# Keys, queries and values of the last attention projected from tiles that carry only their norm weight

## The chip, the cores and the metric

The program runs on one core of one Trainium2 chip. The metric is the device time of one execution in microseconds (us), the median of several. Everything is float32. Five engines work side by side and wait for each other through semaphores: TensorE (PE; its weight loads are listed as PEld), VectorE (DVE), ScalarE (ACT), GpSimd (POOL) and SyncE (SP), which issues most transfers.

## What is computed

The reference is a chain of two transformer blocks of two layers each over 512 tokens of 1024 features. Only the last layer of the second block is touched. It normalises the residual `h` twice, once for keys and values and once for queries, projects, normalises every head of 128, and attends:

```python
def rms_norm(x, g):
    y = x32 * lax.rsqrt(jnp.mean(x32 * x32, axis=-1, keepdims=True) + EPS)
    return (y * g.astype(jnp.float32)).astype(x.dtype)

hn = rms_norm(h, kv_norm)
kv = (hn @ w_kv).reshape(B, S, N_GROUPS, 2, KV_HEADS, HEAD_DIM_2)
k, v = kv[:, :, :, 0], kv[:, :, :, 1]
k = rms_norm(k, k_norm[:, None, :])
...
q = (rms_norm(h, b_norm) @ w_q).reshape(B, S, N_GROUPS, Q_HEADS, HEAD_DIM_2)
q = rms_norm(q, q_norm[:, None, :])
```

A token's factor r = 1/sqrt(mean(h^2) + EPS) passes through the projection. Call the head without it k'. Then the head's own norm gives k' r / sqrt(mean(k'^2) r^2 + EPS) = k' / sqrt(mean(k'^2) + EPS (mean(h^2) + EPS)). So a key or query head needs no factor r: the guard of its root becomes EPS times the token's squared root. A value has no head norm and must be multiplied by r.

## The kernel before

The residual lies in `X`, 8 tiles (k) of 128 features by tokens; columns CTX to TOK are the 512 tokens. The parts of the program that matter here follow each other on TensorE:

- **SW0**, a `fast_stage`: the gated MLP of the layer before. A slot is one weight tile of 1024 KB in a ring of three. `fast_stage` computes a slot as seven products of blocks (Strassen's scheme), numbered 1 to 7; TensorE runs 1, 2, 5, 6, 3, 7, then product 1 of the next slot, then 4. The last four slots (s = 0 to 3) each finish two of the eight tiles of `X`, halves of 256 tokens at a time. DVE does that in `to_residual`: behind product 2, 3 and 7 it adds the product to a copy that ACT made (L1989, L1985), adds the sum to `X` (L1927), squares the half (L1940) and adds the square to a running sum (L1955); behind product 4 it adds straight to `X`. TensorE's product 4 waits for `c22_done`, the add behind product 7.
- **norm(6)**: TensorE multiplies the summed squares by a column of ones (`column`, L793), which gives the sum of each token down a column of PSUM. ACT takes the root (`std`, L1411), DVE the reciprocal (L1832), TensorE spreads it along the partitions (L818), and DVE writes `H` = `X` times weight times root (L1857), one tile at a time. It then copies the spread root to `rstd_s` (L2485) and writes `HKP`, the same product in the order of four phases (L2487).
- **Keys**: three slots of `project` (L665), two units of 8 matmuls each, first from `H`, then from `HKP`. ACT copies a finished unit to `K2` and squares it (`head_tile`, L1713, L1714). The next slot's weights are fetched when an earlier one is done.
- **Values**: three slots of `project_tokens` (L772), copied to `V2` by ACT (L1751). Meanwhile DVE writes `H` anew from `X`, `b_norm` and `rstd_s` (L2518).
- **HEADS**, a `fast_stage` of 12 slots: the query heads. Between products, groups of heads have their squares summed (`group_sums`, `group_turn`), and ACT takes the roots of the collected columns in `small` in three calls of `roots` (L1740): behind slot 1, behind slot 9, and ahead of the attention.
- **dilated_attention**: 32 units in a chain DVE, ACT, TensorE. ACT loads the table of the exponential ahead of the first.

Each engine's program is written out in order by hand; nothing reorders it.

## Time and profile before

| | us |
|---|---|
| median of 3 runs | 3467.29 |
| lowest, highest | 3465.44, 3472.61 |
| the profiled execution | 3469.39 |
| its span, first to last instruction | 3467.8 |

| engine | busy us | share of the span |
|---|---|---|
| PE | 3337.5 | 96% |
| DVE | 2006.7 | 58% |
| POOL | 1019.0 | 29% |
| ACT | 720.5 | 21% |

A matmul in float32 leaves two records in the trace, so a unit of `project` is 16 records. A record's duration overlaps with the next one's; how far apart they start is the cost of a row of them. Matmul times are modelled. Gaps are more telling: a bracket at the end of a row of the timeline is the time in which the engine stood idle ahead of it, and who ended that.

### The profile page before, as it was taken

How to read it: one execution, taken by the hardware profiler on the slowest of the kernel's cores; microseconds unless marked ns; L12 is line 12 of the kernel's file. 1: busy time of each engine (PE TensorE's matmuls, PEld its weight loads, DVE VectorE, ACT ScalarE, POOL GpSimd, SP SyncE). 2: the span in 40 equal slices, each digit the busy share in tenths (PEclk: the TensorE clock that was granted, in tenths of full speed). 3: DMA queues.
4: the chain of work that ended last, by engine and by line, in shares of the span. 5: the costliest groups of instructions: out<-in, count | busy, mean ns of one | idle time of the engine just before them, and what ended most of it. 6: DMA issues, size and time to landing. Idle time of an engine off the chain costs nothing. (4 is left out here: it accounts for less than half of the span.)

```text
span 3467.8 us, 39911 instructions
## 1 busy us (share of the span) xinstructions
PE 3337.5 (96%) x15432; PEld 2475.8 (71%) x15432; DVE 2006.7 (58%) x3518; ACT 720.5 (21%) x1548; POOL 1019.0 (29%) x800
## 2 busy tenths in 40 slices
PE   5999999999999999999999999999999998999998
PEld 4567775555555556778888854888886885678887
DVE  7666467766665443277445657654444676665543
ACT  2243231000101234131111124111111233311110
POOL 0110222322333000223444401344441650234443
PEclk9999999999999999999999999999999999999999
DMA  6332422333321121231222221222222220022222
GB/s 260 108 111 79 114 57 73 118 113 121 116 90 57 65 71 50 70 89 63 88 89 89 87 73 62 75 94 86 85 97 85 80 86 25 26 73 87 93 89 85
DMA packets 63580, 301.70 MB, mean 87 GB/s; under 512 B 7232, under 2 KB 19648, under 8 KB 37280
## 3 DMA queue, kind: packets, MB, share of 16 engines
q1 hardware_dynamic: 51872, 260.87, 22.3%
q0 software_dynamic: 6528, 18.75, 1.7%
q10 hardware_dynamic: 4992, 19.53, 1.5%
q8 instruction: 123, 2.02, 0.2%
q14 instruction: 65, 0.53, 0.1%
HBM read 294.27 MB, written 2.88 MB: 86 GB/s over the span
## 5 line engine op out<-in xcount | busy, mean ns | idle before, releaser
L2580 POOL TENSOR_TENSOR scratch<-ring 128x512 f32<-128x512 f32 (+1 forms) x160 | 214.2, 1339 | 1560.3 <-PE psum L694 1240.9
L694 PE MATMUL psum<-big,scratch 128*128 128x256 f32 (+1 forms) x2240 | 605.6, 426 | 0.0
L694 PEld LDWEIGHTS psum<-big,scratch 128*128 128x128 f32 x2240 | 425.6, 190 | 163.7
L694 PE MATMUL psum<-H,scratch 128*128 128x256 f32 (+1 forms) x2144 | 500.6, 388 | 3.4 <-ACT cb L1344 3.4
L694 PEld LDWEIGHTS psum<-H,scratch 128*128 128x128 f32 x2144 | 405.0, 190 | 84.7 <-ACT cb L1344 8.6
L694 PE MATMUL psum<-big,ring 128*128 128x256 f32 (+1 forms) x1584 | 427.7, 423 | 15.7 <-DVE big L2019 4.9
L665 PE MATMUL psum<-H,ring 128*128 128x512 f32 x928 | 424.2, 608 | 13.4 <-ACT H L1426 11.5
L694 PE MATMUL psum<-H,ring 128*128 128x256 f32 (+1 forms) x1536 | 403.7, 407 | 8.3 <-ACT H L1426 4.2
L694 PEld LDWEIGHTS psum<-big,ring 128*128 128x128 f32 x1584 | 302.6, 192 | 125.8 <-issue 7.2
L694 PEld LDWEIGHTS psum<-H,ring 128*128 128x128 f32 x1536 | 297.4, 194 | 84.4 <-issue 9.4
L665 PEld LDWEIGHTS psum<-H,ring 128*128 128x128 f32 x928 | 175.2, 194 | 222.7 <-issue 217.5
L1344 ACT ACTIVATE cb<-psum 128x256 f32<-128x256 f32 x336 | 128.5, 383 | 849.7 <-PE psum L694 849.7
L2581 POOL TENSOR_TENSOR scratch<-ring 128x512 f32<-128x512 f32 (+1 forms) x160 | 227.4, 1421 | 0.0
L2583 POOL TENSOR_TENSOR scratch<-scratch,ring 128x512 f32<-128x512 f32 (+1 forms) x160 | 225.2, 1407 | 0.0
L2585 POOL TENSOR_TENSOR scratch<-ring,scratch 128x512 f32<-128x512 f32 (+1 forms) x160 | 218.1, 1363 | 12.6
L1344 ACT ACTIVATE big<-psum 128x384 f32<-128x384 f32 x108 | 53.0, 491 | 540.0 <-PE psum L694 540.0
L694 PE MATMUL psum<-X,ring 128*128 128x256 f32 x672 | 159.5, 380 | 3.0 <-DVE cb L1985 1.6
L1989 DVE TENSOR_TENSOR cb<-psum,cb 128x256 f32<-128x256 f32 x104 | 44.0, 423 | 203.0 <-PE psum L694 202.9
L1803 DVE SCALAR_TENSOR_TENSOR big<-big,cb 128x1024 f32<-128x1024 f32 x128 | 158.7, 1259 | 3.1 <-DVE big L1803 2.8
L694 PE MATMUL psum<-X,scratch 128*128 128x256 f32 x672 | 158.7, 379 | 0.0
L2036 DVE TENSOR_TENSOR big<-psum,cb 128x256 f32<-128x256 f32 x88 | 37.2, 422 | 194.7 <-PE psum L694 194.7
L694 PEld LDWEIGHTS psum<-X,ring 128*128 128x128 f32 x672 | 126.7, 190 | 22.4 <-DVE big L1972 2.9
(361 smaller groups left out, 4143.8 us busy)
## 6 DMA issues: line engine op xcount, KB each, us to landing
ring<-in_wall SPq DMA_DIRECT2D x202, 1024.0 KB, 4.9
big<-in_wada SPq DMA_DIRECT2D x48, 512.0 KB, 3.6
big<-in_wada POOLq DMA_DIRECT2D x32, 512.0 KB, 3.9
big<-in_wada ACTq DMA_DIRECT2D x4, 2048.0 KB, 20.1
scratch<-in_rpb ACTq DMA_DIRECT2D x16, 512.0 KB, 4.4
X<-in_xin SPq DMA_DIRECT2D x4, 768.0 KB, 11.9
scratch<-negd SPq DMA_DIRECT2D x8, 384.0 KB, 8.3
big<-negd SPq DMA_DIRECT2D x8, 384.0 KB, 10.9
```

Source lines behind the costliest of these rows:

```text
L665: mm = pe.matmul(acc(w.unit), slot_cols(r, k, f * P, P), rhs_x(k), start=k == 0, stop=k == 7)
L694: mm = pe.matmul(fast_bank(st, q, b), lhsT, rhs(k), start=start and k == 0, stop=k == kt - 1, skip_group_check=True)
L1344: act.activation(piece(st, p, q), fast_bank(st, q, b), ACT.Copy).then_inc(copied[i], 1)
L1803: own(dve.scalar_tensor_tensor(out, w_tile, 1.0, cb[:, j * D:(j + 1) * D], ALU.mult, ALU.mult, accum_out=sums[:, 2 * r + j:2 * r + j + 1]))
L1989: step(dve.tensor_tensor(c, fast_bank(st, q, b), c, ALU.add))
L2036: step(dve.tensor_tensor(GS[s % 2][a], fast_bank(st, q, (0, 2)[x]), piece(st, x, q), ALU.add))
L2580: pool.tensor_tensor(s1, a21, a22, ALU.add).then_inc(combo_own, 1)
L2581: pool.tensor_tensor(s3, a11, a21, ALU.subtract)
L2583: pool.tensor_tensor(s2, s1, a11, ALU.subtract).then_inc(combo_own, 1)
L2585: pool.tensor_tensor(s4, a12, s2, ALU.subtract).then_inc(combos_ready, 1)
```

## The change

Four edits that belong together.

1. The tiles are multiplied by their norm weight alone. DVE writes `H` in `gain_tile`, within the last four slots of SW0: one tile behind the half of product 3, the other behind product 4. `HKP` and, later, the queries' `H` are written by `tensor_scalar` instead of `scalar_tensor_tensor`. The copy to `rstd_s` and the spreading of the root over the partitions (L818, 4 matmuls) are gone.
2. TensorE starts the keys' first slot when the last `c21_done` has come, and sums the tokens' squares behind its first unit (`token_squares`). The sums are now needed in two orders of tokens: 6 columns of 128 tokens, and 12 of 64 tokens, which gather each fourth column of the squares.
3. ACT takes the tokens' roots behind the second unit of keys (`token_roots`). DVE makes EPS times the squared root (the guard) and the reciprocal. `roots` has one instruction for each of the four token blocks, with the guard as bias, where it had one in all.
4. The copy of a value unit is split into two of 256 columns, each scaled by the tokens' reciprocal.

TensorE at the end of SW0 and the start of the keys (`scratch` and `num_b` hold the squares, `con` the identity, `H` and `ring` the operands of `project`):

```order
 L694 MATMUL psum<-big,ring 128x256 x3
-L793 MATMUL psum<-ones,scratch 128x1 x4
-L793 MATMUL psum<-ones,num_b 128x1 x2
-L818 MATMUL psum<-con,small 128x128 x4
-L665 MATMUL psum<-H,ring 128x512 x16
+L665 MATMUL psum<-H,ring 128x512 x8
+L1245 MATMUL psum<-ones,scratch 128x1 x2
+L1245 MATMUL psum<-ones,scratch 64x1 x4
+L1245 MATMUL psum<-ones,scratch 128x1 x2
+L1245 MATMUL psum<-ones,scratch 64x1 x4
+L1245 MATMUL psum<-ones,num_b 128x1 x2
+L1245 MATMUL psum<-ones,num_b 64x1 x4
```

Six sums and four spreading matmuls ahead of the first unit have become eighteen sums between the first and the second.

DVE in the last slot of SW0, from the update of `X` behind product 3, before:

```order
L1985 TENSOR_TENSOR cb<-psum,cb 128x256
L1927 TENSOR_TENSOR X<-cb,X 128x256
L1940 TENSOR_TENSOR aT<-X 128x256
L1955 TENSOR_TENSOR scratch<-scratch,aT 128x256
L1927 TENSOR_TENSOR X<-psum,X 128x256
L1940 TENSOR_TENSOR num_b<-X 128x256
L1832 RECIPROCAL small<-small 128x4
L1857 SCALAR_TENSOR_TENSOR H<-X,vec,psum 128x512 x8
```

and after:

```order
L1991 TENSOR_TENSOR scratch<-scratch,aT 128x256
L2003 TENSOR_SCALAR H<-X,vec 128x512
L2027 TENSOR_TENSOR cb<-psum,cb 128x256
L1963 TENSOR_TENSOR X<-cb,X 128x256
L1976 TENSOR_TENSOR aT<-X 128x256
L1991 TENSOR_TENSOR scratch<-scratch,aT 128x256
L1963 TENSOR_TENSOR X<-psum,X 128x256
L2003 TENSOR_SCALAR H<-X,vec 128x512
L1976 TENSOR_TENSOR num_b<-X 128x256
L2530 TENSOR_SCALAR big<-X,vec 128x512 x8
```

One tile is now written ahead of the add behind product 7 (L2027), one between the last update of `X` and its square.

ACT ahead of the attention (`small` holds the sums of the heads' squares, then their roots), before:

```order
L1729 ACTIVATE big<-psum 128x512
L1735 ACTIVATE small<-psum 128x8
L1740 ACTIVATE small<-small,eps_t 128x24
L1574 ACT_TABLE_LOAD
L1574 ACTIVATE scratch,small<-scratch,small 128x512 x2
```

and after:

```order
L1754 ACTIVATE big<-psum 128x512
L1760 ACTIVATE small<-psum 128x8
L1768 ACTIVATE small<-small 128x6 x4
L1595 ACT_TABLE_LOAD
L1595 ACTIVATE scratch,small<-scratch,small 128x512 x2
```

One root instruction ahead of the table load has become four.

The diff:

```diff
--- before.py
+++ after.py
@@ -1235,8 +1235,28 @@
             fast_stage(SW0)
 
 
-            norm(6)
+            pe.wait_ge(c21_done, w.fast)
             u_k = w.unit
+
+            def token_squares():
+
+                def column(t, at, squares, first=False):
+                    c, n = 6 * 512 + t, squares.shape[-1]
+                    return pe.matmul(psum[at:at + n, c:c + 1], squares, ones[:, 0:1], start=first, stop=True,
+                                     skip_group_check=True)
+
+                def columns(part, a, first=False):
+                    for j in range(2):
+                        column(2 + 2 * a + j, 0, part[:, j * P:(j + 1) * P], first and j == 0)
+                    for q in range(DIL):
+                        mm = column(6 + q, 64 * a, part[:, 0:256].rearrange("p (j q) -> p q j", q=DIL)[:, q, :])
+                    return mm
+
+                pe.wait_ge(sums_made, 6)
+                for a in range(2):
+                    columns(sq_sum[a], a, a == 0)
+                pe.wait_ge(last_squared, 6)
+                columns(sq_part[0], 0).then_inc(ssq_ready, 1)
 
             def group_sums(g):
 
@@ -1278,7 +1298,7 @@
                 if s == 1:
                     pe.wait_ge(h_ready, 8 * 8)
                 project(xq if s == 0 else lambda k: HKP[:, k, :], normed=48 if s == 0 else None,
-                        after=sums_between(0) if s == 2 else None)
+                        after=sums_between(0) if s == 2 else (lambda f: token_squares() if f == 0 else None) if s == 0 else None)
             project_tokens(lambda k, t: H[:, k, t * P:(t + 1) * P], False)
             for s in range(2):
                 project_tokens(lambda k, t: HKP[:, k, (t - CT) * P:(t - CT + 1) * P], False)
@@ -1371,9 +1391,10 @@
                         act.wait_ge(c21_done, q + 1)
                         query_head(q, s, 1)
                         if s == 1:
-                            roots(200, 224)
+                            roots(200, 208, 32)
+                            roots(208, 224).then_inc(q_std, 1)
                         if s == 9:
-                            roots(224, 296)
+                            roots(224, 296).then_inc(q_std, 1)
                     if st.kind == "relu" and kind == "in":
                         act.wait_ge(prod[4], q + 1)
                         act.activation(hid_half(st, 4 + s, 0), fast_bank(st, q, 1), ACT.Relu).then_inc(c21_done, 1)
@@ -1705,7 +1726,11 @@
 
             act.wait_ge(c21_done, w.fast)
             act.dma_start(M2, mask2).then_inc(mask2_in, 16)
-            std(6)
+
+            def token_roots():
+
+                act.wait_ge(ssq_ready, 7)
+                act.activation(small[:, 16:24], psum[:, 3074:3082], ACT.Sqrt, bias=eps_t[:, 0:1], scale=1.0 / D).then_inc(std_done, 1)
 
             def head_tile(i, f):
 
@@ -1736,26 +1761,37 @@
                                bank(7).rearrange("p (t j c) -> p j t c", t=XT, j=4)[:, 0:n, :, 0], ACT.Copy).then_inc(q_cols_out, 1)
                 act.wait_ge(q_cols_out, g + 1)
 
-            def roots(c0, c1):
-                act.activation(small[:, c0:c1], small[:, c0:c1], ACT.Sqrt, bias=eps_t[:, 0:1], scale=1.0 / P).then_inc(q_std, 1)
+            def roots(c0, c1, guard=36):
+
+                cols = small[:, c0:c1].rearrange("p (j t) -> p t j", t=XT)
+                for t in range(XT):
+                    ins = act.activation(cols[:, t, :], cols[:, t, :], ACT.Sqrt, bias=small[:, guard + t:guard + t + 1],
+                                         scale=1.0 / P)
+                return ins
 
             for s in range(3):
                 for f in range(2):
                     head_tile(2 * s + f, f)
+                    if s == 0 and f == 1:
+                        token_roots()
                     if s == 2:
                         (sum_columns if f else sum_rows)(0)
                 w.slot += 1
             for s in range(3):
                 for f in range(2):
                     half(f)
-                    act.activation(V2[:, s, 2 * f:2 * f + 2, :], acc(w.unit).rearrange("p (t c) -> p t c", t=2),
-                                   ACT.Copy).then_inc(acc_free[w.unit % 2], 1)
+                    act.wait_ge(diag_done, 7)
+                    for i in range(2):
+                        c = (24 if s == 0 else 28) + 2 * f + i
+                        ins = act.activation(V2[:, s, 2 * f + i, :], acc(w.unit)[:, 256 * i:256 * (i + 1)], ACT.Copy,
+                                             scale=small[:, c:c + 1])
+                    ins.then_inc(acc_free[w.unit % 2], 1)
                     w.unit += 1
                 w.slot += 1
             fast_stage(HEADS)
             sum_rows(7)
             sum_columns(7)
-            roots(296, 320)
+            roots(296, 320).then_inc(q_std, 1)
             dilated_attention()
             turned_y(8, DT, lambda i: 1.0, False,
                      lambda i, s: (H[:, i, CTX:TOK].rearrange("p (j q) -> p q j", q=DIL),
@@ -1843,7 +1879,7 @@
 
                 if n:
                     inverse(n)
-                dve.wait_ge(rstd_ready, n + 1)
+                dve.wait_ge(rstd_ready, n + 1 - (n > 6))
                 for k in range(DT):
                     if n < 4:
                         a = gain
@@ -1961,6 +1997,12 @@
                                 own.wait()
                                 dve.sem_inc(sums_made, 1)
 
+                def gain_tile(k):
+
+                    if st is SW0:
+                        dve.tensor_scalar(H[:, k, CTX:TOK], X[:, k, CTX:TOK], v("kv_norm", k), None, ALU.mult)\
+                           .then_inc(h_ready, 1)
+
                 def relu2(x):
                     step(dve.scalar_tensor_tensor(x, x, 0.0, x, ALU.max, ALU.mult))
 
@@ -1993,10 +2035,13 @@
                             hook()
                         if last:
                             add_squares(k, a)
+                        if last and i == 3:
+                            gain_tile(2 * s)
                     dve.wait_ge(prod[4], q + 1)
                     to_x(2 * s + 1, 0, fast_bank(st, q, 1)).then_inc(c21_done, 1)
                     if last:
                         dve.wait_ge(c21_done, q + 1)
+                        gain_tile(2 * s + 1)
                         add_squares(2 * s + 1, 0)
 
                 def to_hidden(q, c, s, hook):
@@ -2481,11 +2526,12 @@
             fast_stage(SW0)
 
 
-            norm(6, "kv_norm")
-            own(dve.tensor_copy(rstd_s[:], bank(4)))
             for k in range(DT):
-                dve.scalar_tensor_tensor(phases(HKP[:, k, :]), by_phase(X[:, k, CTX:TOK]), v("kv_norm", k),
-                                         by_phase(bank(4)), ALU.mult, ALU.mult).then_inc(h_ready, 1)
+                dve.tensor_scalar(phases(HKP[:, k, :]), by_phase(X[:, k, CTX:TOK]), v("kv_norm", k), None, ALU.mult)\
+                   .then_inc(h_ready, 1)
+            dve.wait_ge(std_done, 8)
+            own(dve.scalar_tensor_tensor(small[:, 32:40], small[:, 16:24], EPS, small[:, 16:24], ALU.mult, ALU.mult))
+            dve.reciprocal(small[:, 24:32], small[:, 16:24]).then_inc(diag_done, 1)
 
             def rotate(i):
 
@@ -2515,8 +2561,8 @@
 
             dve.wait_ge(half_done, 2 * (w.slot - w.fast + 4))
             for k in range(DT):
-                dve.scalar_tensor_tensor(phases(H[:, k, CTX:TOK]), by_phase(X[:, k, CTX:TOK]), v("b_norm", k),
-                                         by_phase(rstd_s[:]), ALU.mult, ALU.mult).then_inc(hq_ready, 1)
+                dve.tensor_scalar(phases(H[:, k, CTX:TOK]), by_phase(X[:, k, CTX:TOK]), v("b_norm", k), None, ALU.mult)\
+                   .then_inc(hq_ready, 1)
             skip(6, 12)
             mix_input(HEADS, lambda h, j: dve.wait_ge(hq_ready, 4 * h + j + 1))
             for i in (4, 5):
```

## Rows read from the trace of the kernel before

**Rows 1.** Head of the page, and its chain that ended last, by engine
```profile
span 3467.8 us, 39911 instructions
...
PE 13%; DVE 1%; ACT 0%; issue 0%; DVEq 0%; ACTq 0%
```

**Rows 2.** Timeline, TensorE: start, duration, line, tiles, count, idle ahead and releaser
```profile
2612.99 1.56 PE L694 MATMUL psum<-big,ring 128*128 128x256 f32 x6 [0.93 <-DVE cb L1985]
2614.39 1.03 PE L793 MATMUL psum<-ones,scratch 128*128 128x1 f32 x8
...
2620.11 16.02 PE L665 MATMUL psum<-H,ring 128*128 128x512 f32 x32 [0.93 <-DVE H L1857]
2635.97 14.33 PE L665 MATMUL psum<-big,ring 128*128 128x512 f32 x33
```

**Rows 3.** Timeline of the same stretch, ACT and DVE
```profile
2614.59 0.42 DVE L1927 TENSOR_TENSOR X<-psum,X 128x256 f32<-128x256 f32 x1 [0.28 <-PE psum L694]
...
2615.41 1.28 ACT L1411 ACT_TABLE_LOAD   x1 [5.52 <-DVE X L1927]
...
2619.21 5.36 DVE L1857 SCALAR_TENSOR_TENSOR H<-X,vec,psum 128x512 f32<-128x512 f32 x8 [2.03 <-PE psum L818]
...
2625.09 8.44 DVE L2487 SCALAR_TENSOR_TENSOR big<-X,vec,psum 128x512 f32<-128x512 f32 x8
```

**Rows 4.** Windows: stretch, length, busy PE, PEld, DVE, ACT, POOL, granted clock, DMA
```profile
2617.50:2624.20 6.70, 5.77 (x13) 3.23 (x13) 4.99 (x8) 0.00 (x0) 0.00 (x0) 0.50 0.40 169
```

**Rows 5.** Timeline in the fifth norm, and lines: duration ns min/median/max, first and last start
```profile
2013.37 0.36 PE L793 MATMUL psum<-ones,rstd_s 128*128 128x1 f32 x2
...
2015.61 0.36 PE L793 MATMUL psum<-ones,eT 128*128 128x1 f32 x2
...
L1002 PEld LDWEIGHTS psum<-big x608: 132/137/138, 183.9 to 1408.2; 128*64 128x64 f32 x152
...
L847 PE MATMUL psum<-small,con x32: 197/198/218, 150.1 to 151.0; 64*64 64x6 f32 x32
```

**Rows 6.** Timeline of SW0's last four slots, all engines
```profile
2594.07 1.26 POOL L2580 TENSOR_TENSOR scratch<-ring 128x384 f32<-128x384 f32 x1 [4.65 <-PE psum L694]
...
2595.65 1.10 DVE L1940 TENSOR_TENSOR aT<-X 128x256 f32<-128x256 f32 x1
...
2601.74 0.42 DVE L1989 TENSOR_TENSOR cb<-psum,cb 128x256 f32<-128x256 f32 x1 [0.54 <-PE psum L694]
...
2602.83 4.05 PE L694 MATMUL psum<-big,ring 128*128 128x256 f32 x18
...
2603.46 0.42 DVE L1985 TENSOR_TENSOR cb<-psum,cb 128x256 f32<-128x256 f32 x1
...
2610.80 0.42 DVE L1989 TENSOR_TENSOR cb<-psum,cb 128x256 f32<-128x256 f32 x1 [2.08 <-PE psum L694]
```

**Rows 7.** Line L2284: a multiplication by a column, SBUF to SBUF, ns
```profile
L2284 DVE TENSOR_SCALAR wx<-wx,small x32: 485/486/488, 173.4 to 1393.8; 128x512 f32<-128x512 f32 x32
```

**Rows 8.** Timeline where the values end and HEADS begins, ACT and TensorE
```profile
2706.71 0.60 ACT L1751 ACTIVATE big<-psum 128x512 f32<-128x512 f32 x1 [6.31 <-PE psum L772]
...
2707.40 3.69 PE L694 MATMUL psum<-H,ring 128*128 128x256 f32 x16 [0.73 <-issue]
```

**Rows 9.** Timeline of ACT within HEADS, behind slot 1
```profile
2736.84 0.30 ACT L1740 ACTIVATE small<-small,eps_t 128x24 f32<-128x24 f32 x1
2738.67 0.38 ACT L1344 ACTIVATE wx<-psum 128x256 f32<-128x256 f32 x1 [1.53 <-PE psum L694]
```

**Rows 10.** Timeline ahead of the attention's first transpose, ACT and TensorE
```profile
2876.66 0.18 ACT L1735 ACTIVATE small<-psum 128x8 f32<-128x8 f32 x1 [2.12 <-PE psum L1260]
2876.87 0.31 ACT L1740 ACTIVATE small<-small,eps_t 128x24 f32<-128x24 f32 x1
2877.20 1.28 ACT L1574 ACT_TABLE_LOAD   x1
...
2879.36 0.66 PE L1066 MATMUL psum<-con,scratch 128*128 128x128 f32 x4 [2.74 <-ACT scratch L1574]
```

## What the change was predicted to do, and why

> **What bounds the kernel now.** I read the page's chain first: PE is the only engine in it with a share worth the name, and the span is 3467.8 us [rows 1]. The profiled execution took 3469.39, 2.1 above the median of the three runs (3467.29), so a difference found on the profile is taken off the median. Since TensorE is busy almost all the time, a time can only be won where it stands idle or runs at a lower clock, and is lost wherever something is put into its stream. So I read TensorE's timeline around the norm that the change removes, with the other engines beside it, and then the places where the change adds work: the end of SW0, the copy of the last value unit, and the roots.
>
> The last product of SW0 starts at 2612.99 and ends at 2614.55; the first matmul of the keys starts at 2620.11 [rows 2]. That is 5.56 us without useful work. In it lie one chain: DVE's last update of `X` (2614.59 to 2615.01), its square, ACT's table load and root, the reciprocal, the spreading matmuls, the first tile of `H` at 2619.21 [rows 3]. Two more microseconds go behind it: the first 32 records of the keys take 16.02 us, while the 33 of the next slot take 14.33 [rows 2], so 32 should take 13.9. The reason is in the windows: the granted clock is 0.50 from 2617.5 to 2624.2, which is the 1.2 GHz level [rows 4]. It fell after TensorE had had only the short sums and nothing else for 3 us.
>
> **The change, part by part.**
>
> *Gap.* TensorE now waits for the last update of `X` alone, which ends at 2615.01 [rows 3]. Seven of eight tiles of `H` are ready by then; the eighth is written right behind and is needed only after seven matmuls of 2 x 0.43 us (14.33 over 33 records [rows 2]). I allow 0.1 us for the wait, so the first matmul starts at 2615.1 in place of 2620.11: minus 5.0 us.
>
> *Clock.* The idle time left is 0.56 us. Ahead of HEADS TensorE stands idle 0.73 us [rows 8] and runs on at its pace (16 records in 3.69 us). So I take the 2.1 us of the lower clock as won: minus 2.1 us, between 0 and 2.1.
>
> *The tokens' sums in TensorE's stream.* Before, six sums lay in the gap; now eighteen stand between two units that had none between them. A sum of 128 tokens costs what the fifth norm shows: ten starts apart from 2013.37 to 2015.61, so 0.224 us each [rows 5], and six make 1.34 us. A sum of 64 tokens is not in the trace. Its weights are 64 columns wide and gather every fourth float; a 64-wide load from 128 partitions takes 137 ns [rows 5], and a 128-wide pair costs 0.224. From above I bound it by 0.33 us (a whole sum and half as much again, should the gathering slow it), from below by 0.06, which is the 16 small matmuls of L847 in 0.94 us [rows 5]. I take 0.16, scaled by the load's 137 ns against the 192 of the 128-wide loads, which are the larger part of 0.224. Twelve make 1.9 us. Together plus 3.3 us, between 2.1 and 5.3. The Trainium skill (TensorE: Matmul & The Clock Gate, section LDWEIGHTS) says that a weight load goes by its number of columns alone, P / 1.2 ns. By it a half-wide sum would cost half a whole one, twelve would make 1.3 us, and the sum of all terms below would be 0.6 us lower; the 64-wide load's 137 ns [rows 5] is well over half of a whole one's, so I do not go by it.
>
> *DVE at the end of SW0.* Each of the last four slots gets two `tensor_scalar` of 512 elements. Such a one takes 0.486 us [rows 7]. TensorE waits for DVE at product 4, for the add behind product 7. In the last slot it already waits 0.93 us [rows 2], so the tile written ahead of that add costs its full 0.5. In the third slot the add runs from 2603.46 to 2603.88, and product 4 is due three matmuls (6 of 18 records) behind 2602.83, at 2602.83 + 4.05 / 3 = 2604.2 [rows 6]: 0.3 of slack against 0.5, and DVE had 0.54 idle ahead of that slot's chain [rows 6] to take up the second tile. The second slot is alike. The first slot has no running sum to add to yet, so its add comes about 0.4 earlier and hides the tile. With DVE some tenths late from the second tile of the slot ahead: 0 + 0.4 + 0.4 + 0.5 = plus 1.3 us. Bounds: 0.9, if nothing is handed on, to 2.8, if the tiles of the first two slots meet GpSimd's `tensor_tensor`s (L2580 at 2594.07), beside which a DVE square takes 1.10 us where it takes 0.42 elsewhere [rows 6]. The last slot's 2.08 us idle [rows 6] stops it from growing further.
>
> *Phases.* `HKP`'s eight operations took 8.44 us from 2625.09 [rows 3] and now start some 9 us earlier; TensorE wants them behind sixteen matmuls of the first slot. Nothing. The same holds for the queries' `H`.
>
> *Tokens' roots.* ACT loads the table (1.28 us [rows 3]) between two copies of key units that are 6.9 us apart. Nothing.
>
> *Values.* Each copy becomes two of 256. Such copies take 0.38 [rows 9], a whole one 0.60 [rows 8]. Five hide behind the next unit; the last is what TensorE waits for ahead of HEADS [rows 8]: plus 0.2 us.
>
> *Roots in HEADS.* Behind slot 1 one instruction of 0.30 us becomes eight, about 2 us of ACT, where the next copy came after 1.53 us of idle [rows 9]. That copy may be 0.3 late; TensorE asks for it one product later. Nothing.
>
> *Roots ahead of the attention.* These do lie on the path: root 2876.87, table load 2877.20, exponential, transpose at 2879.36 after 2.74 us of idle on TensorE [rows 10]. Three more small instructions at 0.2 us, the pitch of the two small ones there (2876.66 to 2876.87): plus 0.6 us, between 0.4 and 0.9.
>
> Sum: -5.0 - 2.1 + 3.3 + 1.3 + 0.2 + 0.6 = -1.7 us. That gives 3467.29 - 1.7 = 3465.6. With the lower bounds the sum is -5.0 - 2.1 + 2.1 + 0.9 + 0.2 + 0.4 = -3.5, with the upper ones -5.0 + 5.3 + 2.8 + 0.2 + 0.9 = +4.2 (the clock not won).
>
> **The rivals.**
>
> *A: the clock falls anyway.* It fell 3 us behind the last large matmul although twelve records of sums ran in between [rows 2, 4], so such sums may not count as work for it, and the block of eighteen is about 3.3 us long. Against it: full matmuls stand on both sides without a gap. Then the 2.1 us are paid behind the block and the sum is +0.4: 3467.7.
>
> *B: DVE becomes the bound of SW0's end.* If the tiles take about 1.1 us, as the square beside GpSimd does [rows 6], term four grows to 2.8 or more and with the second tiles handed on to about 3.5. The sum is +0.5: 3467.8. For it speaks a rule of the Trainium skill (Advanced Engine Details and Errata): the second SBUF port of VectorE is shared with GpSimd, and two-port VectorE instructions and GpSimd's block each other. The trace shows the slow square beside L2580, but GpSimd works only in the first two of the four slots, so by that rule two slots are hit, not four.
>
> *C: slower than before, by the gathered sums.* If a weight load that picks every fourth float costs 0.33 us or more per sum, the block reaches 5.3 us, more than the gap it stands in for. The trade turns at a block of 5.0 us, 1.7 more than I take, if the clock stays up, and at 2.9 if it falls behind the block. With both, -5.0 + 5.3 + 1.3 + 0.8 = +2.4: 3469.7. No row shows a gathered weight load, so I cannot exclude it.
>
> *D: the change does not do what it says*, because something else still holds the keys back. The weights of their first slot are there (TensorE did not wait for them), and the listing of the order shows the norm's wait gone. I leave 0.02 for it: time as before or some tenths above.
>
> **How the numbers follow.** Forecast 0.58, A 0.17, B 0.12, C 0.09, D 0.02, and 0.02 for what I have not seen. The terms reach from -3.5 to +4.2; the three runs of before lie within 7 us of each other, their median is uncertain by about 2. The range 3462.5 to 3471 takes in all cases with that. A measurement of this kernel can tell about 0.2%, 6.9 us, from no change. All named cases lie within it, so: faster 0.04, same 0.93, slower 0.03, where both ends are only for a chain in HEADS or the attention that turns out longer or shorter than the rows say.
>
> **What would show it.** In the profile of the changed kernel: TensorE's idle time between SW0's last product and the keys about 0.6 us, with the granted clock at 1.00 there; the first unit in 6.9 us; a block of sums of 3.3 us, 36 records; product 4 waiting for the add behind product 7 in the last three slots, 0.4 to 0.5 us more each; `tensor_scalar` at 0.49 us; idle of TensorE 0.9 us ahead of HEADS and 3.3 us ahead of the attention's first transpose. I am wrong if the block of sums is under 2 or over 5 us, if the clock falls behind it, or if anything in HEADS waits that did not.

## The result, and the profile after

| | before | after |
|---|---|---|
| median us | 3467.45 (20 runs) | 3472.23 (20 runs) |
| lowest to highest | 3463.53 to 3472.61 | 3469.0 to 3478.66 |
| the profiled execution, its span | 3469.39, 3467.8 | 3470.63, 3469.0 |

The changed kernel takes 1.0015 of the time, 95% interval 1.0009 to 1.0021: 4.8 us more. That is under the 0.2% set above, but the interval leaves no doubt about the sign. I had forecast 3465.6, 1.7 less than before, and the measured time lies outside the range.

The medians are the measure here. The two profiled executions differ by less. The one of after was already 1.9 us ahead where these slots begin (2582.79 for the product that starts at 2584.70 before), ahead of anything that the change touches; so I compare stretches, not the starts.

TensorE's timeline from the first of SW0's last four slots to the keys' third unit (start, duration, line, tiles, count, idle ahead and releaser), the answer to [rows 2] and [rows 6]:

```profile
2584.77 2.86 PE L694 MATMUL psum<-big,ring 128*128 128x256 f32 x12 [0.52 <-DVE cb L2027]
...
2594.88 2.86 PE L694 MATMUL psum<-big,ring 128*128 128x256 f32 x12 [0.78 <-DVE cb L2027]
...
2602.75 4.35 PE L694 MATMUL psum<-big,ring 128*128 128x256 f32 x18
...
2613.61 1.56 PE L694 MATMUL psum<-big,ring 128*128 128x256 f32 x6 [1.33 <-DVE cb L2027]
2615.69 7.13 PE L665 MATMUL psum<-H,ring 128*128 128x512 f32 x16 [0.52 <-DVE X L1963]
2622.66 3.13 PE L1245 MATMUL psum<-ones,scratch 128*128 128x1 f32 x24
2625.72 1.96 PE L1245 MATMUL psum<-ones,num_b 128*128 128x1 f32 x12
2627.60 9.64 PE L665 MATMUL psum<-H,ring 128*128 128x512 f32 x16
2637.08 20.76 PE L665 MATMUL psum<-big,ring 128*128 128x512 f32 x48
```

The gap is gone: from the start of the last product to the first matmul of the keys are 2.08 us, where [rows 2] has 7.12. The first unit costs 6.97 us to the start of the sums. The sums take 4.94 us (2622.66 to 2627.60), and the second unit 9.48 (2627.60 to 2637.08) in place of 6.9. In SW0's last four slots TensorE waits for DVE's add in the first two where it had not, loses 0.30 us in the third and waits 0.40 us longer in the last.

The windows show why the second unit is slow (length, busy PE, PEld, DVE, ACT, POOL, granted clock, DMA):

```profile
2617.00:2625.00 8.00, 8.00 (x33) 4.76 (x31) 4.25 (x8) 1.18 (x2) 0.94 (x2) 1.00 0.47 195
2625.00:2626.00 1.00, 1.00 (x9) 0.98 (x9) 0.00 (x0) 0.00 (x0) 0.10 (x1) 0.93 0.33 66
2626.00:2632.00 6.00, 6.00 (x16) 3.42 (x17) 0.00 (x0) 0.00 (x0) 0.00 (x0) 0.50 0.00 0
2632.00:2633.00 1.00, 1.00 (x3) 0.53 (x2) 0.00 (x0) 0.00 (x0) 0.00 (x0) 0.65 0.00 0
```

The granted clock is 1.00 (the 2.4 GHz level) through the gap and the first unit and falls to 0.50 (1.2 GHz) within the block of sums, from about 2625.9 to 2632.7. TensorE is busy in every one of these windows. In [rows 4] the low stretch stood behind the norm; now it stands behind the sums.

DVE and GpSimd in the first of SW0's last four slots, and DVE in the third:

```profile
2583.14 1.25 DVE L2003 TENSOR_SCALAR H<-X,vec 128x512 f32<-128x512 f32 x1
...
2583.10 1.00 POOL L2626 TENSOR_TENSOR scratch<-ring 128x384 f32<-128x384 f32 x1 [5.34 <-PE psum L694]
...
2603.38 0.48 DVE L2003 TENSOR_SCALAR H<-X,vec 128x512 f32<-128x512 f32 x1
```

The tile written ahead of the add takes 1.25 us beside GpSimd and 0.48 without it; in the second slot the same pair stands at 2593.27 (1.22) and 2592.95.

The values and the attention, the answers to [rows 8] and [rows 10]:

```profile
2708.76 3.69 PE L694 MATMUL psum<-H,ring 128*128 128x256 f32 x16 [0.98 <-issue]
...
2878.25 0.89 ACT L1768 ACTIVATE small<-small 128x6 f32<-128x6 f32 x4
...
2881.32 0.66 PE L1066 MATMUL psum<-con,scratch 128*128 128x128 f32 x4 [3.31 <-ACT scratch L1595]
```

0.25 us more ahead of HEADS, 0.57 more ahead of the first transpose. Within HEADS the eight roots hide: the copy behind them still finds 0.22 us of idle, where [rows 9] had 1.53.

```profile
2738.19 1.61 ACT L1768 ACTIVATE small<-small 128x2 f32<-128x2 f32 x8
2740.02 0.38 ACT L1364 ACTIVATE wx<-psum 128x256 f32<-128x256 f32 x1 [0.22 <-PE psum L694]
```

Added up: gap -5.0, old low clock -1.9, sums +4.9, new low clock +2.5, waits in SW0 +2.5 (worked out below), values +0.25, attention's start +0.6. That is +3.8 of the 4.8 us, and the interval of the whole reaches from 3.1 to 7.3. The old low clock is 1.9 and not 2.1 because the first 32 records take 15.86 us from start to start [rows 2]; 16.02 is the row's duration, which overlaps with the next. Of the 4.9 for the sums some 0.35 belongs to the low clock too: the last twelve records take 1.88 us, while two sums of 128 and four gathered ones cost 1.53 at clock 1.00 (prices below).

Two more differences lie between the two profiles, and I can't put them down to the change. From its first transpose to the transposes behind it (L1180) the attention takes 108.0 us before and 109.0 in the changed kernel, but in the runs below that have the changed kernel's attention it takes 108.1 to 109.8. And the first 16 records of the products behind the attention take 5.38 us before, where the granted clock is 0.57 from 2996 to 3000, and 3.69 in the changed kernel.

### The profile page after: what moved, and what is told of

It is laid out like the page before. It is cut to its first block and busy times, and to the rows that moved or that the text cites. A ratio compares the mean times of both kernels' runs of the same rounds, so it can differ in the third digit from the quotient of the medians.

```text
span 3469.0 us, 39968 instructions
## 1 busy us (share of the span) xinstructions
PE 3340.9 (96%) x15448; PEld 2477.6 (71%) x15448; DVE 1998.5 (58%) x3518; ACT 724.3 (21%) x1567; POOL 1015.2 (29%) x800
```

## The experiments

Every kernel ran 11 times, with before beside it on the same chip. "Theory 1" in the first expectations is the account above. Two limits hold for all that follows. Where a median is set against the changed kernel's 3472.23, two chips are compared, and before's own median lies between 3467.45 and 3468.75 on them. And what is said of the granted clock is read from one profiled execution of each kernel.

| kernel | median us | before on that chip | ratio, 95% interval |
|---|---|---|---|
| one sum | 3463.61 | 3468.07 | 0.9984 (0.9975 to 0.9993) |
| gathering undone | 3469.59 | 3468.07 | 1.0007 (0.9998 to 1.0016) |
| sums spread | 3473.17 | 3468.07 | 1.0016 (1.0008 to 1.0025) |
| first tile later | 3469.65 | 3468.07 | 1.0005 (0.9996 to 1.0014) |
| eight sums | 3466.6 | 3467.99 | 0.9994 (0.9985 to 1.0003) |
| eight sums, tiles on ACT | 3464.49 | 3467.99 | 0.9986 (0.9977 to 0.9995) |
| tiles on ACT | 3469.97 | 3467.99 | 1.0005 (0.9996 to 1.0014) |
| two blocks of nine | 3472.14 | 3468.75 | 1.0007 (0.9998 to 1.0016) |
| roots and values undone | 3470.09 | 3468.75 | 1.0007 (0.9998 to 1.0015) |
| block behind the second unit | 3474.0 | 3468.16 | 1.0017 (1.0008 to 1.0027) |

**One sum.** The block is cut to a single sum of 128 tokens:

```diff
-                for a in range(2):
-                    columns(sq_sum[a], a, a == 0)
                 pe.wait_ge(last_squared, 6)
-                columns(sq_part[0], 0).then_inc(ssq_ready, 1)
+                column(2, 0, sq_part[0][:, 0:P], True).then_inc(ssq_ready, 1)
...
-                act.activation(small[:, 16:24], psum[:, 3074:3082], ACT.Sqrt, bias=eps_t[:, 0:1], scale=1.0 / D).then_inc(std_done, 1)
+                act.activation(small[:, 16:24], psum[:, 3074:3075].to_broadcast([P, 8]), ACT.Sqrt, bias=eps_t[:, 0:1], scale=1.0 / D).then_inc(std_done, 1)
```

> The changed kernel with one of its eighteen sums in the tokens' block instead of all; ACT takes the root of that one sum eight times, so the tokens' factors are wrong. Everything waits as before. Theory 1 (the block of 36 records, 4.94 us in the changed kernel's profile, makes the clock fall behind it, and both are the loss): the block shrinks to about 0.3 us, the granted clock stays at 1.00 in the keys' first slot, its second unit takes 6.9 us instead of 9.5, and the time falls by 4.6 + 2.6 = 7.2 us against the changed kernel, to some 2 to 3 us under the kernel before. Theory 2 (the clock falls because of the idle 0.5 us and the waits at the end of SW0, not of the sums): it still falls in the first slot, only 4.6 us are won, about level with the kernel before. Theory 3 (most of the loss is in the end of SW0 or in the roots): less than 4 us are won.

TensorE's timeline, and one window over both units and beyond (columns as above):

```profile
2618.80 0.28 PE L1245 MATMUL psum<-ones,num_b 128*128 128x1 f32 x2
2618.94 7.11 PE L665 MATMUL psum<-H,ring 128*128 128x512 f32 x16
```

```profile
2618.00:2640.00 22.00, 22.00 (x54) 9.86 (x53) 6.83 (x11) 5.25 (x9) 2.97 (x6) 1.00 0.18 57
```

The block costs 0.14 us, the clock stays up, the second unit takes 6.95 us (7.11 less the overlap of its last record, as the next starts at 2625.89). By rows this saves 4.94 - 0.14 + 9.48 - 6.95 = 7.3 us; the median is 8.6 below that of the changed kernel. The loss sits in the block and in what it does to the clock.

**Gathering undone.** Each sum of 64 tokens reads 64 neighbouring columns in place of every fourth, so the later roots belong to other tokens; number and width of the sums are the same.

```diff
-                        mm = column(6 + q, 64 * a, part[:, 0:256].rearrange("p (j q) -> p q j", q=DIL)[:, q, :])
+                        mm = column(6 + q, 64 * a, part[:, 64 * q:64 * q + 64])
```

> The changed kernel with the twelve 64-wide sums reading 64 neighbouring columns of the squares instead of each fourth one (the phases' sums are those of other tokens). In the changed kernel four 128-wide and eight 64-wide sums took 3.06 us, which leaves 0.27 us for a 64-wide one. Theory 1a (gathering makes the load slow): a 64-wide sum falls to 0.12 to 0.16 us, the block to about 3.3 us, and the clock may then stay at 1.00: 1.6 to 4 us won. Theory 1b (a 64-wide load or the narrower output has a cost of its own, gathered or not): the block stays at 4.9 us, nothing changes.

```profile
2622.25 2.15 PE L1245 MATMUL psum<-ones,scratch 128*128 128x1 f32 x24
2624.33 1.18 PE L1245 MATMUL psum<-ones,num_b 128*128 128x1 f32 x12
2625.44 8.76 PE L665 MATMUL psum<-H,ring 128*128 128x512 f32 x16
```

The first 24 records are four sums of 128 and eight of 64. From start to start they take 2.08 us here and 3.06 in the changed kernel, at clock 1.00 in both. Four times 0.224 off, a sum of 64 costs (2.08 - 0.90) / 8 = 0.15 us near and (3.06 - 0.90) / 8 = 0.27 gathered. The gathering costs 0.12 us a sum, and it lies in the weight load. The loads of the sums of 64, in the changed kernel and then here (busy us, mean ns of one), beside 190 ns for those of 128 in both:

```profile
L1245 PEld LDWEIGHTS psum<-ones,scratch 128*64 128x64 f32 x16 | 2.1, 213 | 0.0
...
L1245 PEld LDWEIGHTS psum<-ones,scratch 128*64 128x64 f32 x16 | 1.1, 137 | 0.0
```

The block is 3.19 us now, and the clock still falls:

```profile
2625.00:2626.00 1.00, 1.00 (x9) 0.92 (x9) 0.00 (x0) 0.00 (x0) 0.00 (x0) 0.67 0.26 41
2626.00:2628.00 2.00, 2.00 (x3) 0.67 (x2) 0.00 (x0) 0.00 (x0) 0.00 (x0) 0.50 0.00 0
```

So even with a block as short as the 3.3 us of the forecast, the clock term would have failed. The second unit takes 8.60 us here: the clock is low for 3.4 us, where it was low for 6.8 in the changed kernel. By rows 1.75 + 0.88 = 2.6 us are won, and so say the medians.

**Sums spread.** One sum ahead of each matmul of 512 columns, from the third matmul of the keys on, so that no block is left; the tokens' roots come behind the third unit.

```diff
...
+                        if k < 8:
+                            each(f, k)
                         mm = pe.matmul(acc(w.unit), slot_cols(r, k, f * P, P), rhs_x(k), start=k == 0, stop=k == 7)
...
```

> The changed kernel with the eighteen sums one at a time between the matmuls of the keys' first three units (from the third matmul on) instead of in one block; the tokens' roots are taken behind the third unit. The work is the same. Theory 1 (it is the block as a block that lets the clock fall): the clock stays at 1.00 through the first slot; at an unchanged cost per sum 2.6 us are won. If besides the sums' weight loads hide behind the 512-column matmuls, whose own loads leave the loader idle for 0.24 us in each 0.43, another 1 to 3 us are won. Theory 2 (the clock falls for another reason): it falls as before, at about the same time after the start of the keys, and nothing or only the hidden loads are won.

```profile
2621.23 0.40 PE L1247 MATMUL psum<-ones,scratch 128*64 128x1 f32 x2
...
2622.61 0.40 PE L1247 MATMUL psum<-ones,scratch 128*64 128x1 f32 x2
...
2626.36 0.28 PE L1247 MATMUL psum<-ones,scratch 128*128 128x1 f32 x2
```

```profile
2616.00:2640.00 24.00, 24.00 (x75) 11.37 (x75) 5.30 (x10) 2.35 (x4) 1.99 (x4) 1.00 0.34 120
```

The clock stays up, and yet nothing is won. A matmul with a gathered sum takes 1.38 us (2621.23 to 2622.61), a matmul alone 0.87 (13.9 us over 16), so the sum costs 0.51, not 0.27. A sum of 128 costs 0.21. From the first sum at 2617.59 to the matmul behind the last at 2639.71 are 22.1 us with 17 matmuls at 0.87, so the eighteen sums cost some 7.4 us: as much as block and low clock together (4.94 + 2.5). Parting the sums gives back the clock and takes it again at each of them.

**First tile later.** The tile that `gain_tile` writes behind product 3 is written behind product 7's halves instead, so that the add for which TensorE waits goes ahead of it.

```diff
-                        if last and i == 3:
+                        if last and i == 7:
                             gain_tile(2 * s)
```

> The changed kernel with the first tile of each of SW0's last four slots written behind the squares of product 7 instead of ahead of the add that product 4 waits for. In the changed kernel those tiles cost TensorE 0.78 + 1.04 + 0.30 + 0.40 = 2.5 us in the four slots. Theory A (it is the place ahead of the add): product 4 waits no more than in the kernel before, about 2 us won. Theory B (it is DVE's total work in a slot): the next slot's adds come as late as now, and at most 0.7 us are won, in the last slot.

```profile
2593.08 2.86 PE L694 MATMUL psum<-big,ring 128*128 128x256 f32 x12 [0.61 <-DVE cb L2027]
...
2611.12 1.56 PE L694 MATMUL psum<-big,ring 128*128 128x256 f32 x6 [0.94 <-DVE cb L2027]
```

The waits of the first and third slot are gone, the last one is back at 0.94 (0.93 before), and one of 0.61 is left in the second; theory A holds in the main, and why the second slot still waits stays open. How much the waits cost is read from the distance between like rows: without a wait a slot repeats after 9.07 us (2598.36 to 2607.43 in the kernel with the tiles on ACT and eight sums, below); in the changed kernel the second slot takes 10.11 (2587.46 to 2597.57) and the third 9.37. With 0.78 for the first slot and 0.40 for the last the sum is 2.5 us; here 0.9 is left. The median is 2.6 us lower. By rows it is these 1.6 us and 1.1 of the clock (block 4.64, second unit 8.67): in this execution it fell only 4.9 us behind the block's start, where it had been 3.2, and was low for 3.4 us. One execution doesn't tell whether the edit did that or the moment.

**Eight sums.** DVE adds the last tile's squares to the running sum and copies the sums, in the order of the phases, to the free `rstd_s`; TensorE then makes four sums in one order and four in the other, all 128 wide and none gathered. Nothing of the computation is left out.

```diff
-                pe.wait_ge(sums_made, 6)
-                for a in range(2):
-                    columns(sq_sum[a], a, a == 0)
-                pe.wait_ge(last_squared, 6)
-                columns(sq_part[0], 0).then_inc(ssq_ready, 1)
+                pe.wait_ge(phased, 2)
+                for t in range(XT):
+                    column(2 + t, 0, sq_sum[t // 2][:, (t % 2) * P:(t % 2 + 1) * P], t == 0)
+                for q in range(XT):
+                    mm = column(6 + q, 0, rstd_s[:, q * P:(q + 1) * P])
+                mm.then_inc(ssq_ready, 1)
...
+            dve.wait_ge(last_squared, 6)
+            dve.wait_ge(sums_made, 6)
+            step(dve.tensor_tensor(sq_sum[0][:, 0:256], sq_sum[0][:, 0:256], sq_part[0][:, 0:256], ALU.add))
+            for a in range(2):
+                dve.tensor_copy(rstd_s[:].rearrange("p (q j) -> p q j", q=DIL)[:, :, 64 * a:64 * a + 64],
+                                sq_sum[a][:, 0:256].rearrange("p (j q) -> p q j", q=DIL)).then_inc(phased, 1)
```

> The changed kernel with eight sums of 128 neighbouring columns in the block instead of eighteen: DVE first adds the last tile's squares to the running sum and copies the sums into the order of the phases, in time that it has free; nothing of the computation is left out. At 0.112 us a record the block should take 16 records, 1.8 us. Theory 1 (the length of the block lets the clock fall: 4.94 us did and 3.19 us did, 0.28 us did not): between these I cannot say, I expect 1.00 throughout, and 3.1 + 2.6 = 5.7 us less than the changed kernel, about 3466.5 and 1 to 2 us under the kernel before. If the clock falls nevertheless, the second unit takes 8 us or more and only 3 to 4 us are won. Theory 2 (a sum's cost is not in its load): the block keeps over 0.2 us for each record pair more than the fifth norm shows, and less than 3 us are won.

```profile
2623.16 0.95 PE L1246 MATMUL psum<-ones,scratch 128*128 128x1 f32 x8
2623.97 1.03 PE L1246 MATMUL psum<-ones,rstd_s 128*128 128x1 f32 x8
2624.86 7.11 PE L666 MATMUL psum<-H,ring 128*128 128x512 f32 x16
```

```profile
2616.00:2640.00 24.00, 23.81 (x68) 11.61 (x69) 10.88 (x22) 5.02 (x8) 2.15 (x5) 1.00 0.33 120
```

The block is 1.70 us, the clock stays 1.00, the second unit takes 6.95. By rows 3.2 + 2.5 = 5.8 us less than the changed kernel, by the median 5.6. DVE's add (0.42 us) and copies (0.69 each) hide behind the first unit. Here the gather is done by the engine that has time for it.

**Tiles on ACT.** ACT, which has time at the end of SW0, multiplies the eight tiles of `H` by their weight, behind the slot's halves; DVE no longer does. Alone, and together with the eight sums:

```diff
+                    if st is SW0 and st.last(kind, g):
+                        for k, done in ((2 * s, c12_done), (2 * s + 1, c21_done)):
+                            act.wait_ge(done, q + 1)
+                            act.activation(H[:, k, CTX:TOK], X[:, k, CTX:TOK], ACT.Copy, scale=v("kv_norm", k))\
+                               .then_inc(h_ready, 1)
...
-                        if last and i == 3:
-                            gain_tile(2 * s)
...
-                        gain_tile(2 * s + 1)
...
+            dve.wait_ge(h_ready, 56)
```

> The changed kernel with the eight tiles of H on ACT as in the run before, and the eighteen sums left as they are. Alone this should give back the 2.5 us of product 4's waits (late tiles on DVE gave 1.9 us in the profile), with the block at 4.9 us and the clock falling behind it as before: about 3469.7, still above the kernel before. If it brings less than 1 us, ACT has taken DVE's place as the engine waited for.

> The eight sums of the run before, and besides the eight tiles of H written by ACT (an activation with the norm weight as scale) instead of DVE in SW0's last four slots; nothing is left out. Product 4 should then wait no more than in the kernel before, 2.5 us less than with the tiles on DVE: theory 1 gives some 3464, 3.5 to 4.5 us under the kernel before. Rival: ACT's activations stand ahead of its copy of product 5 and make product 3 wait for that; then less than 1.5 us of the 2.5 come.

Of the two together, TensorE:

```profile
2603.54 4.05 PE L695 MATMUL psum<-big,ring 128*128 128x256 f32 x18
2607.43 5.34 PE L695 MATMUL psum<-big,scratch 128*128 128x256 f32 x24
2613.70 1.56 PE L695 MATMUL psum<-big,ring 128*128 128x256 f32 x6 [0.93 <-DVE cb L2027]
```

The end of SW0 reads as in [rows 2] again: 0.93 us in the last slot and no wait ahead of it. An ACT tile takes 0.72 us where DVE took 0.48, and nobody waits for it. Together the two edits are 7.7 us below the changed kernel by the medians (by rows 5.8 + 2.5) and 3.5 us below before, with an interval that excludes 1. The full change with its sums and tiles placed so beats both kernels. The clock stays at 1.00 behind its block of 1.71 us too. Tiles on ACT alone took 2.3 us off the changed kernel, where rows give 2.5 for the waits and 0.4 for a shorter low clock.

In the run with the tiles on ACT alone the clock fell sooner, 2.3 us behind the block's start (2621.49), where it fell 3.2 us behind it in the changed kernel:

```profile
2623.00:2624.00 1.00, 1.00 (x9) 0.99 (x9) 0.00 (x0) 0.00 (x0) 0.93 (x2) 0.91 0.00 0
2624.00:2630.00 6.00, 6.00 (x22) 4.01 (x22) 0.00 (x0) 0.00 (x0) 0.00 (x0) 0.50 0.06 11
```

**Two blocks of nine**, behind the first and the second unit, to see whether the length of a block is all that counts. The sums are the same; nine are taken at a time, four of 128 and five gathered ones of 64 in the first block, two and seven in the second.

> The changed kernel with its 18 sums of squares of a slot in two blocks of nine: the first block (two of the three steps of four tokens and one more sum) behind the first key unit, the second behind the second unit, the tokens' roots behind the third unit. Nothing else is changed, and all 18 sums are taken. Theory 1 (what lets the clock fall is the length of an unbroken block of one-column products; in the runs so far it fell behind blocks of 3.19 and 4.94 us and stayed up behind 0.28 and 1.70 us): each block takes about 2.4 us, the granted clock stays 1.00 from the first unit to the third, both following units take about 7.1 us, and the kernel is about 2.6 us faster than the changed one (about 3469.6 us where that has 3472.2). Rival (any 18 such sums within these units lower the clock, however they are parted): the granted clock falls to 0.50 behind one of the two blocks and the unit behind it takes 9 us or more; no gain.

```profile
2621.28 2.42 PE L1245 MATMUL psum<-ones,scratch 128*128 128x1 f32 x18
2623.62 8.83 PE L665 MATMUL psum<-H,ring 128*128 128x512 f32 x16
2632.39 0.88 PE L1245 MATMUL psum<-ones,scratch 128*64 128x1 f32 x6
2633.19 1.65 PE L1245 MATMUL psum<-ones,num_b 128*128 128x1 f32 x12
2634.77 20.44 PE L665 MATMUL psum<-big,ring 128*128 128x512 f32 x47
```

```profile
2624.00:2625.00 1.00, 1.00 (x2) 0.33 (x1) 0.00 (x0) 0.00 (x0) 0.00 (x0) 0.57 0.27 43
...
2628.00:2640.00 12.00, 12.00 (x41) 6.44 (x40) 0.00 (x0) 1.17 (x2) 0.96 (x2) 1.00 0.27 94
```

The rival came out, if with 8.77 us where it said 9: behind the first block (2.34 us) the clock falls and is low for 3.4 us; behind the second (2.38 us) it stays up. By rows 0.8 us is won against the changed kernel; the median shows 0.1. In these two blocks the length does not decide. Nor can a length be read from the others: with the tiles on ACT alone the clock had fallen after 2.3 us of sums, with the late tile only after 4.9.

**Block behind the second unit.** All 18 sums one unit later, to see whether the idle time of TensorE at SW0's end counts together with the first block.

```diff
-(lambda f: token_squares() if f == 0 else None) if s == 0
+(lambda f: token_squares() if f == 1 else None) if s == 0
...
-                    if s == 0 and f == 1:
+                    if s == 1 and f == 0:
                         token_roots()
```

> The changed kernel with its block of 18 sums moved from behind the first key unit to behind the second, and the tokens' roots from behind the second unit to behind the third. Nothing else is changed. With the sums in two blocks of nine the granted clock fell behind the first block (2.34 us, one unit behind the idle time at SW0's end) and stayed up behind the second (2.38 us). Theory 2 (what counts with the sums is the idle time of TensorE at SW0's end, one unit ahead of them): the whole block stands two units behind that idle time, 14 us, and the granted clock stays 1.00 or falls for clearly less than in the changed kernel; the unit behind the block takes under 8 us in place of 9.5, and the kernel is about 2 us faster than the changed one. Rival (a block of this length lets the clock fall wherever it stands, and two blocks of nine lie at the edge): the granted clock falls to 0.50 in or behind the block for about 7 us, the unit behind it takes about 9.5 us, and the time is that of the changed kernel, about 3472.

```profile
2622.04 14.00 PE L665 MATMUL psum<-H,ring 128*128 128x512 f32 x32 [0.52 <-DVE X L1963]
2635.88 3.13 PE L1245 MATMUL psum<-ones,scratch 128*128 128x1 f32 x24
2638.94 2.06 PE L1245 MATMUL psum<-ones,num_b 128*128 128x1 f32 x12
2640.93 23.25 PE L665 MATMUL psum<-big,ring 128*128 128x512 f32 x48
```

```profile
2640.00:2644.00 4.00, 4.00 (x12) 2.42 (x13) 0.00 (x0) 0.00 (x0) 0.00 (x0) 0.50 0.11 41
```

The rival again (the window has the clock at 0.50). The block takes 5.05 us, the clock falls as before, and the 48 records behind take 23.25 us in place of 20.76: 2.5 us, the same price 14 us behind the idle time where it had been 7. So the idle time is not needed for the fall, against theory 2. Why one block of nine lowered the clock and the other did not stays open; besides their place they differ in their mix of sums, and each was seen once.

**Roots and values undone.** The roots of the heads are one instruction each with a constant guard, the values are copied whole; the token's guard and the tokens' factor of the values are left out of the computation.

```diff
-                for t in range(XT):
-                    ins = act.activation(cols[:, t, :], cols[:, t, :], ACT.Sqrt, bias=small[:, guard + t:guard + t + 1],
-                                         scale=1.0 / P)
+                return act.activation(small[:, c0:c1], small[:, c0:c1], ACT.Sqrt, bias=eps_t[:, 0:1], scale=1.0 / P)
...
-                    for i in range(2):
-                        c = (24 if s == 0 else 28) + 2 * f + i
-                        ins = act.activation(V2[:, s, 2 * f + i, :], acc(w.unit)[:, 256 * i:256 * (i + 1)], ACT.Copy,
-                                             scale=small[:, c:c + 1])
+                    ins = act.activation(V2[:, s, 2 * f:2 * f + 2, :], acc(w.unit).rearrange("p (t c) -> p t c", t=2), ACT.Copy)
```

> The changed kernel with the two small parts of the change undone: the roots of the heads are one instruction each again with a constant guard (the token's guard is left out of the computation), and the values are copied whole and unscaled (the tokens' factor of the values is left out). The 18 sums and the clock stay as in the changed kernel. Theory 1 (these parts cost what their rows show): the wait of TensorE ahead of the attention's first transpose goes from 3.31 back to about 2.74 us (0.6 less), the idle time ahead of the heads' first product behind the values goes from 0.98 back to about 0.73 us (0.25 less), the whole is about 0.8 us less than the changed kernel, which medians can hardly show. Rival (the two parts cost more than these two waits, for example in the work of ScalarE beside the attention): the median falls by 2 us or more, and other waits in the heads' part shorten.

```profile
2710.34 3.69 PE L694 MATMUL psum<-H,ring 128*128 128x256 f32 x16 [0.73 <-issue]
...
2882.31 0.66 PE L1066 MATMUL psum<-con,scratch 128*128 128x128 f32 x4 [2.74 <-ACT scratch L1594]
```

Both waits have their old size, 0.73 and 2.74 us, so these two places cost 0.25 and 0.57 us, as their rows said, and between them nothing else changes (171.97 us against 172.56, the 0.57 less). The median is 2.1 us lower than the changed kernel's, and 3.4 if each is taken against before on its own chip; the rival had asked for 2. Its place for the rest would be the attention, which takes 108.2 us here and 109.0 in the changed kernel, but 108.1 with the two blocks, where the roots are in. So whether these parts cost more than 0.8 us stays open.

## Why the prediction was wrong, point by point

- **Gap: right.** -5.0 forecast, -5.0 measured; 0.52 us of idle.
- **Clock: the step that failed.** I took the 2.1 us as won (1.9 from start to start) because hardly any idle time was left. The fall at the norm is gone, as said. But I priced the sums as time only, though [rows 4] and rival A said that a stretch of sums had lowered the clock before. The block of this very change lowered it, and the second unit paid 2.5 us. "Full matmuls stand on both sides" was no protection. With the gathering undone the block had about the length that I had forecast, and the clock fell too. So in place of -2.1 this step comes to -1.9 + 2.5 = +0.6.
- **The tokens' sums: term mis-sized.** +3.3 forecast, +4.9 measured, inside the bounds. The sum of 64 was taken at 0.16 us. That is right for neighbouring columns (0.15), but the gathered one costs 0.27; the nearest row had no gathering in it. Rival C's point of "2.9 us if the clock falls" was passed. The Trainium skill (TensorE: Matmul & The Clock Gate, section LDWEIGHTS) says that a weight load goes by its columns alone. This trace doesn't agree: loads of the same 64 columns take 213 ns gathered and 137 near, and the measurement decides.
- **DVE at the end of SW0: mechanism right, slots wrong.** +1.3 forecast, +2.5 measured. In the last two slots the terms came out at 0.30 and 0.40. In the first two, which I had put at 0 and 0.4, they were 0.78 and 1.04, since the tile lies beside GpSimd: 1.25 and 1.22 us in place of 0.48. That is rival B's mechanism, near my upper bound of 2.8. I had it in the bounds and took the other end, though rival B itself says that GpSimd works in the first two slots ([rows 6] show it in the second). The rule of the Trainium skill that is cited there (Advanced Engine Details and Errata, section VectorE Performance Modes) says that such instructions and GpSimd's block each other. The slow `tensor_scalar` in two slots of four agrees with it.
- **Phases, tokens' roots, roots in HEADS: right,** all hidden. `HKP` takes 4.85 us (it took 8.44) and is early; the tokens' roots lie between two copies.
- **Values and attention: right,** +0.25 and +0.57 for +0.2 and +0.6.
- **The combination.** A came true, with most of B and of C's price. I gave each a chance as if they excluded each other and priced C's corner at 3469.7 without B's full size. Nothing kept them apart, so their errors add up. The range was too narrow for that even by my own bounds: the upper ones give 3467.29 + 4.2 = 3471.5, and the range ended at 3471. The measured terms give 3467.45 + 3.8 = 3471.3; for the last 0.9 us to 3472.23 I have no row that I can put down to the change.

## What to carry to other kernels

When small products leave a gap and enter the stream of an engine that is the bound, price them twice: their own time, with the layout that they really read, and what a stretch of them does to the granted clock; then look for an engine with idle time that can shrink them, as DVE did here with three operations. Work added to a second engine in the tail of a stage should be placed by what runs beside it and by who waits on the instruction behind it, not by its length alone. Spreading small products between large ones is not free and has to be measured like a block.

## What the runs showed of the hardware

- A one-column float32 product costs 0.224 us with 128 weight columns, 0.15 with 64 neighbouring ones and 0.27 with 64 that lie four apart (weight loads of 190, 137 and 213 ns); between matmuls of 512 columns the first costs 0.21 and the last 0.51.
- The granted clock falls with TensorE busy throughout: in or behind blocks of one-column products of 3.19, 4.64, 4.94, 5.03, 5.05 (twice) and (once) 2.34 us, 2.3 to 4.9 us behind the block's start. It stayed at 1.00 with blocks of 2.38, 1.70, 1.71 and 0.14 us and with eighteen products one at a time. The low stretch lasted 3.4 or 6.8 us, and the unit behind took 1.7 to 2.5 us longer.
- DVE's `tensor_scalar` of 128x512 takes 0.48 us and beside GpSimd's `tensor_tensor` 1.22 to 1.25.
